# Input projections from high and low parts in both layers of a streaming encoder

## The reference, cut to what matters

```python
for l in range(DEPTH):
    h = x * (1.0 + sc1) + sh1
    z = h @ w_in[l]
    a_u, a_v, b_cq, b_ckv, b_kr, c_u, d_q, d_f, d_i, d_g = jnp.split(z, IN_SPLITS, axis=-1)
    y_a = spatial_gating(gelu(a_u), gelu(a_v), ...)
    y_b = mla(b_cq, b_ckv, b_kr, ...)          # latent attention, 4 heads
    y_c = s5(c_u, ...)                         # diagonal state space, 16 groups
    y_d = hgrn2(d_q, d_f, d_i, d_g, ...)       # gated linear recurrence, chunks of 64
    ym = rms_norm(concatenate([y_a, y_b, y_c, y_d]))
    x = layer_norm(DN_ALPHA * x + (1.0 + g1) * (ym @ w_out[l]), ...)
    h = x * (1.0 + sc2) + sh2
    x = layer_norm(DN_ALPHA * x + (1.0 + g2) * conv_ffn(h, w_up, ..., w_down), ...)
```

## Time and profile before

| | before |
|---|---|
| median of 3 runs | 1365.28 us (1364.83 to 1368.31) |
| profiled execution | 1366.21 us |
| its span, first to last instruction | 1364.3 us |
| mean granted clock of PE | 0.976 |
| PE busy | 1318.7 us, 97% |
| DVE busy | 878.7 us, 64% |
| ACT busy | 513.7 us, 38% |
| POOL busy | 217.5 us, 16% |
| input projections of layer 0 | about 49 to 250 us of the span |
| input projections of layer 1 | about 713 to 906 us |

### The profile page before, as it was taken

One profiled execution on the slowest core, in us unless ns is written; L12 is line 12 of the kernel. 1 busy time (PEld: TensorE's weight loads), 2 busy tenths in 40 slices (PEclk: granted clock), 3 DMA queues, 4 the chain that ended last, 5 costly groups with the idle time before them and its releaser, 6 DMA issues.

```text
span 1364.3 us, 17249 instructions
## 1 busy us (share of the span) xinstructions
PE 1318.7 (97%) x6866; PEld 998.8 (73%) x6866; DVE 878.7 (64%) x1523; ACT 513.7 (38%) x770; POOL 217.5 (16%) x193
## 2 busy tenths in 40 slices
PE   6899999999999999999999999999999999999997
PEld 3445777786788888888865576867778888888886
DVE  5985777856877777868562647476675555553335
ACT  2523223433633334434225422253363333343323
POOL 0640200633200000000039010043340000000003
PEclk9998999998999999999989999999999999999998
DMA  9455643022566666755315142102223333333331
GB/s 387 169 123 170 145 139 114 27 78 77 170 192 195 196 189 196 255 206 178 93 50 133 53 86 59 32 17 78 62 93 95 104 95 93 96 105 93 93 93 62
DMA packets 64801, 166.79 MB, mean 122 GB/s; under 512 B 14288, under 2 KB 26960, under 8 KB 64208
## 3 DMA queue, kind: packets, MB, share of 16 engines
q1 hardware_dynamic: 64720, 165.68, 39.6%
HBM read 160.04 MB, written 5.62 MB: 121 GB/s over the span
## 4 chain that ended last, share of the span: by engine, by line
PE 83%; DVE 11%; DMA 2%; issue 2%; POOL 1%; ACT 1%; SPq 0%; ACTq 0%; POOLq 0%; DVEq 0%
PE bank L498 18%; PE bank L499 18%; PE bank L500 18%; PE bank L589 8%; PE bank L583 3%; PE bank L614 2%; PE bank L518 1%; PE bank L513 1%; PE bank L742 1%; PE bank L779 1%; PE bank L507 1%; PE bank L1022 1%; DVE xa L1161 1%; PE bank L761 1%; PE bank L751 1%
## 5 line engine op out<-in xcount | busy, mean ns | idle before, releaser
L498 PE MATMUL bank<-ym_r,scr_r 128*128 128x512 f32 x688 | 268.7, 391 | 4.9 <-DVE hm_r L1787 2.5
L499 PE MATMUL bank<-ym_r,ring_r 128*128 128x512 f32 x688 | 267.8, 389 | 0.0
L500 PE MATMUL bank<-hm_r,scr_r 128*128 128x512 f32 x688 | 267.7, 389 | 0.0
L1230 DVE TENSOR_TENSOR ring_r<-ring,scr_r 128x1024 fp32r<-128x1024 f32 x134 | 165.6, 1236 | 88.8 <-ACT scr_r L1942 88.6
L1942 ACT ACTIVATE scr_r<-ring 128x1024 fp32r<-128x1024 f32 x146 | 153.4, 1052 | 133.9 <-DMA ring<-in_w_down 109.4
L498 PE MATMUL bank<-scr_r 128*128 128x512 f32 x480 | 188.5, 393 | 2.1 <-DVE ym_r L1723 2.0
L499 PE MATMUL bank<-scr_r,ring_r 128*128 128x512 f32 x480 | 187.1, 390 | 0.0
L589 PE MATMUL bank<-hm,ring 128*128 128x512 f32 x336 | 165.9, 636 | 0.0
L498 PEld LDWEIGHTS bank<-ym_r,scr_r 128*128 128x128 f32 x688 | 129.1, 188 | 36.7 <-issue 6.2
L500 PEld LDWEIGHTS bank<-hm_r,scr_r 128*128 128x128 f32 x688 | 129.1, 188 | 27.0
L499 PEld LDWEIGHTS bank<-ym_r,ring_r 128*128 128x128 f32 x688 | 129.2, 188 | 26.1
(11 more groups left out here) (370 smaller groups left out, 1782.9 us busy)
## 6 DMA issues: line engine op xcount, KB each, us to landing
ring<-in_w_up SPq DMA_DIRECT2D x88, 512.0 KB, 3.7
ada<-in_w_ada SPq DMA_DIRECT2D x80, 512.0 KB, 3.7
ring<-in_w_down SPq DMA_DIRECT2D x44, 512.0 KB, 3.6
ring<-in_w_in SPq DMA_DIRECT2D x33, 512.0 KB, 4.7
scr<-in_w_ada SPq DMA_DIRECT2D x16, 512.0 KB, 14.1
ring<-in_w_out SPq DMA_DIRECT2D x16, 512.0 KB, 3.6
pa<-in_par_a SPq DMA_DIRECT2D x2, 2144.5 KB, 12.9
xa<-in_x SPq DMA_DIRECT2D x1, 2048.0 KB, 8.4
```

What stands on the lines that cost most here:

```text
L498: first = mm(dst, w_hi, x_hi, start=start, stop=False)
L499: mm(dst, w_lo, x_hi, start=False, stop=False)
L500: return first, mm(dst, w_hi, x_lo, start=False, stop=stop)
L1230: V.tensor_tensor(ring_r[:, slot(l, n), :], ring[:, slot(l, n), :], high[:, slot(l, n), :].bitcast(F32), ALU.subtract)\
```

## The change

From Q0 on in layer 0 (10 chunks) and from F0 on in layer 1 (14 chunks), `project` goes to `project_split`, which uses `thrice`. For it:

- ACT makes the high part of each such chunk (`win_made`), into two slots in layer 0 (a part of `pa` that has been used, and the new `win_high`), and three in layer 1 (`ada` twice and `silu_c`). It waits until the chunk that had the slot is done.
- DVE makes the low part in place in the ring (`win_low`), at places written out in its list; in layer 0 POOL makes five of them (G1, AV0, AV1, AU0, AU1).
- ACT copies the tiles of `hm` into `xa` as fp32r (`tiles_made`), and DVE takes the difference in place in `hm` (`tiles_split`), once the last fp32 chunk has read each tile. So `xa` is first stored to DRAM (`stream`, two DMAs ahead of chunk 4 on SP), and loaded again after the last projection, ahead of the fourth output chunk.
- The token chunks are computed with channels on partitions like the others, evicted (`tok_in`), turned by four transposes on PE (`turn_tokens`) and evicted again (`evict_turned`). `hg_update(0)` and `hg_update(1)` move one projection part back.
- Semaphores are merged to make room, some small tables and a margin of unused memory go, and four small tiles move to the end of the memory.

```diff
+FIRST_SPLIT = [AT[Q0], 3]
+POOL_WIN = [[AT[j] for j in (G1, AV0, AV1, AU0, AU1)], []]
...
+        win_high = [[pa_r[:, spare:spare + SLOT], win_r[:, :]], [ada_r[:, 0, :], ada_r[:, 1, :], silu_r[:, :]]]
...
+                def project_split(p, part):
+                    bank = banks[p % 2]
+                    if part == 0:
+                        name, count = low_made(l, p)
+                        pe.wait_ge(S[name], count)
+                        if p >= 4:
+                            pe.wait_ge(S["proj_out"], l * NPROJ + p - 1)
+                    w_hi, w_lo = (a.rearrange("p (k m) -> p k m", m=P) for a in (high_slot(l, p), ring_r[:, slot(l, p), :]))
+                    for k in ((0, 1, 2), (3, 4, 5), (6, 7))[part]:
+                        if p == FIRST_SPLIT[l]:
+                            pe.wait_ge(S["h_lo"], tiles_low(l, 0) + k + 1)
+                        first, last = thrice(bank[:, :], w_hi[:, k, :], w_lo[:, k, :], xa_r[:, k, :], hm_r[:, k, :],
+                                             k == 0, k == KD - 1)
+                        if k == 0:
+                            first.then_inc(S["chunk_used"], 2 if p == (2 if l == 0 else 3) else 1)
+                    if part == 2:
+                        last.then_inc(S["proj_mm"], 1)
...
                 project(AT[G0], 0)
-                hg_update(0)
+                turn_tokens(AT[I1])
+                if AT[I1] not in split_win(l):
+                    hg_update(0)
                 project(AT[G0], 1)
+                if AT[I1] in split_win(l):
+                    hg_update(0)
                 attend(9)
                 project(AT[G0], 2)
-                hg_update(1)
+                if AT[I1] not in split_win(l):
+                    hg_update(1)
                 project(AT[G1], 0)
+                if AT[I1] in split_win(l):
+                    hg_update(1)
...
+            def win_low(l, j):
...
+                v.wait_ge(S["w_hi"], high_made(l, p))
+                V.tensor_tensor(ring_r[:, slot(l, p), :], ring[:, slot(l, p), :], high_slot(l, p).bitcast(F32), ALU.subtract)\
+                    .then_inc(S["w_lo_dve"], 1)
...
+            def tiles_split(l):
...
+                for k in range(KD):
+                    v.wait_ge(S["h_hi"], tiles_high(l, 0) + k + 1)
+                    if k < KD - 1:
+                        v.wait_ge(S["pe_tile"], 2 + splits_below(l) * (KD - 2) + max(k, 1))
+                    else:
+                        v.wait_ge(S["proj_mm"], l * NPROJ + FIRST_SPLIT[l])
+                    V.tensor_tensor(hm_r[:, k, :], hm[:, k, :], xa_r[:, k, :].bitcast(F32), ALU.subtract).then_inc(S["h_lo"], 1)
...
+            def win_made(l, j):
...
+                ahead = len(win_high[l])
+                a.wait_ge(landed[slot(l, p)], landings(l, p))
+                if p - FIRST_SPLIT[l] >= ahead:
+                    a.wait_ge(S["chunk_used"], l * NCHUNK + p + 5 - ahead)
+                A(high_slot(l, p), ring[:, slot(l, p), :], ACT.Identity).then_inc(S["w_hi"], 1)
...
+                for p in POOL_WIN[l]:
+                    g.wait_ge(S["w_hi"], high_made(l, p))
+                    G.tensor_tensor(ring_r[:, slot(l, p), :], ring[:, slot(l, p), :], high_slot(l, p).bitcast(F32), ALU.subtract)\
+                        .then_inc(S["w_lo"], 1)
```

More of the change, by code:

```diff
@@ L47 @@
 NPROJ = 17
+TOKENS = [I0, I1, AV0, AV1]
 WIN = [CQ0, CQ1, CKV, F0, F1, U0, U1, Q0, Q1, I0, I1, G0, G1, AV0, AV1, AU0, AU1]
@@ L342, in trunk, with high_slot, token_tile @@
         }
+        x_d = nc.dram_tensor("stream", [P, KD, T], F32).ap()
+        spare = PA_AT["w_uq"][0]
+        win_high = [[pa_r[:, spare:spare + SLOT], win_r[:, :]], [ada_r[:, 0, :], ada_r[:, 1, :], silu_r[:, :]]]
+        def high_slot(l, p):
+            return win_high[l][(p - FIRST_SPLIT[l]) % len(win_high[l])]
+        def token_tile(p):
+            if WIN[p] == AV0:
+                return avt[:, :, P:2 * P]
+            tile = qh[:, 0, :] if WIN[p] == AV1 else ym[:, 3, :]
+            return tile.rearrange("p (b t) -> p b t", t=P)
         def inner(k):
@@ L1648, in _ @@
                 attend(11)
+                win_low(l, AV0)
                 level(2)
@@ L1668, in _ @@
                 level(8)
+                win_low(l, AU1)
                 level(9)
@@ L1982, in evict @@
                     tok = bank[:, :].rearrange("p (b n) -> p b n", n=P)
+                    if j in TOKENS and p in split_win(l):
+                        A(token_tile(p), tok, ACT.Identity).then_inc(S["tok_in"], 1)
+                        return
                     if j in (U0, U1):
@@ L2003, in evict, with evict_turned @@
                     ins.then_inc(S["proj_out"], 1)
+                def evict_turned(p):
+                    if p not in split_win(l):
+                        return
+                    j = WIN[p]
+                    a.wait_ge(S["tok_mm"], splits_below(l) * 4 + TOKENS.index(j) + 1)
+                    dst, c = (vtok, j - I0) if j in (I0, I1) else (avt, j - AV0)
+                    A(dst[:, :, c * P:(c + 1) * P], banks[p % 2][:, :].rearrange("p (b n) -> p b n", n=P), ACT.Identity)\
+                        .then_inc(S["proj_out"], 1)
                 def level_exp(s):
@@ L2118, in _ @@
                 evict(AT[AV0])
+                win_made(l, AU0)
                 attend(14)
+                evict_turned(AT[AV0])
                 attend(15)
@@ L2123, in _ @@
                 evict(AT[AV1])
+                win_made(l, AU1)
                 attend(16)
+                evict_turned(AT[AV1])
                 level_exp(9)
```

180 lines of the change are left out of this document (139 added, 41 removed).

## The result

The changed kernel takes 1373.69 us (median of 5, 1371.32 to 1374.35), the kernel before 1365.28 on the same chip: ratio 1.0065, 95% interval 1.0037 to 1.0092. It is slower by 0.65%, where I forecast 0.3% faster. The profiled execution has a span of 1371.9 us, 7.6 more than before.

A forecast was written before the change was run, and what follows sets the result against it. PE was taken to bound by little, with DVE right behind; of 34 us off PE, layer 0's +1.1 and layer 1's -5.5 summed to -4.4, a median of 1360.9. The forecast's own range was 1355 to 1366, the full range 1347 to 1371.

The forecast's parts named there:

- (a), (b): Layer 0: low part and eight tiles on DVE before first attention block, +6.1; PE then bounds to I0, -2.3.
- (c): Layer 0, I0: no gain, since PE waits for DVE, DVE for POOL, POOL for the S5 kernel transfer.
- (d), (e): Layer 0: G0's low part costs DVE 0 up to 199 us; POOL's five low parts cost DVE +3.
- (f), (g): Layer 0 from 200 us, where PE bounds: AV0 and AV1 give -3.3, AU0 and AU1 -2.4.
- (i) to (l): Layer 1: up to first attention block +0.4; Q0, Q1 -2.8; I0 and part of I1 -1.7; G0's low part +0.8.
- (m): Layer 1, G1: its low part on DVE and first part on PE come between the state updates, +3.2.
- (n): Layer 1, PE up to 852 us: three quarters of a chunk saved, but DVE follows with two more low parts, -0.5.
- (o), (p), (q): Layer 1's end: AV0 and AV1 give -3.3, AU0 and AU1 -2.4; two late low parts on DVE cost +0.8.
- D: Rival: fp32r on these operands runs at fp32's pace, so a chunk is not cheaper; 1378, chance 0.03.
- B: Rival, the clock: four longer waits on PE cost 1.8 each, POOL's parts 8 instead of 3; 1373, chance 0.22.
- A: Rival: DVE has more room than forecast, its added work and POOL's parts being hidden; 1348, chance 0.20.
- C: Rival, nothing arrives: layer 1 loses at U0 and G1 what it wins; 1365, chance 0.10.

The follow-up runs named there:

- layer 1 with GpSimd: Against the kernel before, only layer 1 is split and GpSimd makes its low parts of G1, AV0, AV1, AU0, AU1: 1359.03 us, ratio 0.9971.
- the first kernel without low parts: The change with only 8 of 1024 columns of each weight low part made, high parts read instead: 1360.83 us, 0.9971 of the kernel before.

## Why the prediction was wrong

The forecast was 1360.9 and the result 1373.7. Measured in the profiled executions, in the order of the steps:

- **(a), (b)** were right: +6.2 where I had +6.1, then -3.0 where I had -2.3. (c) was 1.0 where I had 0.
- **(d), (e)** failed. I had 0 for G0's low part and +3, a quarter of 12 us, for all of POOL's five parts. The first of them and G0's low part moved the first state update of layer 0 from +4.2 to +7.4, of which the run without GpSimd's parts puts 2.05 on the lock; the rest, 1.2, goes to G0's low part, for which PE waits 2.41 us, and to the part of G0 that now stands ahead of the update. I had 0 for both, from DVE's free time in the whole window and not from where it lies. By the S5 outputs it is +9.8, so 5.6 where the two steps had 3. Three of POOL's five parts stretched an instruction, 6 us of DVE's time; half, not a quarter. (The pair of rows 7 that I took as the lock's price was itself too dear: its two products take 2.1 us alone, not 1.29.) Between 176 and 194 three half-clock stretches follow where there was one.
- **(f), (g)** gave 3.5 of 5.7: from +9.8 at the S5 outputs (196.80 before) to +6.3 at the last levels (250). Layer 0 so ends 6.3 us late instead of 1.1. The run of layer 0 alone puts its price at 4.5.
- **(i) to (l)** were right in sum: from 700 to the first state update the change wins 1.5 us; the steps add up to -3.3, and the update now stands behind one part more, 2.0.
- **(m)** was named with its cause and its chain, and mis-sized: 3.2 forecast, 4.9 measured between the updates, since the part runs at half clock (3.7 us, not 2.04). Taking the chain apart was worth 0.4 to 0.5%, 5 to 7 us.
- **(n)** failed: -0.5 forecast, +2.3 measured from the second update to 852, though the update stands behind one part more and PE had that much less to do behind it. The step took it that PE bounds there; the second states came 5.1 us late, and PE waited for them.
- **(o), (p), (q)** failed. They add up to -4.9; from 852 to 901 the change wins 4.3, and then gives 3.6 back by 937. The steps took it that PE bounds once the mixers end. There PE waits for DVE, which stands behind POOL's lock at the gate's product, a row that I had read and used only as a price for (e). The lock and a wait of 0.92 were there before; what the change adds is 0.8 of wait, and a granted clock of 0.88 instead of 0.95. Moving the product takes 0.42% off the change.
- **The ceiling** held for fp32r: matmuls at full clock start 0.23 us apart, so D is out. Three take 0.69 and not 0.68, which makes the 34 us some 32. They became 21.5 off PE's busy time. The forecast took the clock as it was; it gave back 8.
- **The range** of 1347 to 1371 was said to take in most of B, whose own number is 1373. It did not; the result lies 2.7 above it.

In sum the profile is 12 us above my -4.4: 5.2 from layer 0 up to its last levels, 6.3 from layer 1 up to 852 (of it 4.8 behind the second update, by (n) and the part that (i) to (l) left open), 4.2 from there to 937 and 0.9 behind it, less the 4.6 that came back between 250 and 700, where the clock was granted at 1.00 instead of 0.98 and which no step had. So the step that failed most is the claim that PE bounds behind the places where it waits for DVE.

Of the rivals, B (1373) has the number, and the four longer waits at the named places, 2.7 + 4.2, 2.4, 2.2 and 4.0 us, and POOL's parts nearer to 6 than to 3. But that each such wait costs 1.8 us by half clock is wrong for two of the four, G0 and U0, behind which PE ran at full clock; the clock took its 8 us at other places as well, and the run that filled three of the waits took half-clock stretches away and no time. So B's number is in part luck. I gave B 0.22 because DVE would hide PE's slow parts; at G1 the part stands in a chain that returns to PE, and nothing hides it. A is out. C had layer 1 right, which gains nothing, but not layer 0.

Of the signs that I named, the 4 us at G1 came as written, the DVE adds over 2 us did, and PE idles 29 us more. The idle time at Q0 came in two pieces, 2.73 us ended by DVE and 4.15 ended by ACT, which had itself waited 6.56 for DVE. PE's busy time fell by less than 30, and DVE was busy 36.02 of 40 us in layer 0, not 38. The clock's fall from 0.976 to 0.970 is B's sign only in part: the 8 us are in the result, and I had not said how far under is well under.

## What to carry to other kernels

When work moves from the bounding engine to one that it waits for, don't sum free time by window: follow each moved instruction to the point where its result is wanted, and look for a chain that returns to the first engine. Here one such chain of five links cost 5 to 7 us, and moving one statement out of it gave 5 of them back. The same splitting in layer 1 alone, with the chain cut, the second part of G1 ahead of level 1, and the gate's product where DVE idles, takes 1352.6 us, 0.85% less than the kernel before. And a profile of one execution is not the place to settle 5 us: the clock put that much between two executions of the same code, so ratios over several runs decide, and the profile only says where.

## What the runs showed of the hardware

- The half clock does not sit at fixed places of a program. In one execution it took 7% of the full-speed time between 104 and 200 us, in another of the same instructions nothing. One and the same wait of 2.4 us was followed by it in two profiles of seven.
- Executions of one kernel differ in time as they differ in clock. On one chip the kernel before took 1356.86 us at a mean granted clock of 0.985 and 1369.20 at 0.972.
- The kernels with split projections were granted less than the kernel before, by the means over all their runs: 0.970 for the change, 0.971 and 0.973 for the two without low parts, 0.974 for layer 1 with GpSimd and 0.977 for the fastest kernel, against 0.978 to 0.979. It does not follow the speed: the change and the first kernel without low parts are 0.9% apart in time and 0.001 in clock.
- A GpSimd instruction of 2.4 to 2.6 us stretches a 0.42 us instruction of DVE on two SBUF inputs to 2.3 to 2.5, and leaves the state update, which reads PSUM, at its 3.61.
